# Gate matrices of eight tokens instead of four, one batch per two slabs, with one set of one-hot buffers filled in halves

## What is computed

```python
def block(xt):                                   # 8 heads, 128 x 128 experts, top 16 per head
    q = (xt @ w_q).reshape(T, PEER_HEADS, 2, PEER_HALF)
    s = jnp.einsum('thpd,hpkd->thpk', q, sub_keys)
    s_top, i_top = lax.top_k(s, PEER_TOPK)       # best 16 of each half
    ...                                          # best 16 sums of a pair (i1, i2): eid = i1 * 128 + i2
    gate = jax.nn.softmax(best, axis=-1)
    u_sel, v_sel = jnp.take(u_tab, eid, axis=0), jnp.take(v_tab, eid, axis=0)
    act = jax.nn.gelu(jnp.einsum('td,thkd->thk', xt, u_sel), approximate=False)
    return jnp.einsum('thk,thkd->td', gate * act, v_sel)
```

## Time and profile before

| | us |
|---|---|
| runs, median of 3 | 3200.51 (3197.85 to 3203.13) |
| profiled execution, its own time | 3202.34 |
| its span, first to last instruction | 3200.5 |
| PE busy | 3004.4 (94%) |
| DVE busy | 2184.9 (68%) |
| ACT busy | 1586.0 (50%) |
| POOL busy | 964.1 (30%) |
| gate matmuls (L627), 4608 of them | 200.2 busy |

### The profile page before, as it was taken

How to read it: one execution, slowest core, us unless ns; L and a number is a source line. 1 busy time by engine, 2 the same in 40 slices (tenths; PEclk the granted TensorE clock), 3 DMA queues, 4 the chain that set the end, 5 groups by cost and what they waited for, 6 DMA issues and landing times.

```text
span 3200.5 us, 66478 instructions
## 1 busy us (share of the span) xinstructions
PE 3004.4 (94%) x22938; PEld 2712.0 (85%) x22938; DVE 2184.9 (68%) x4296; ACT 1586.0 (50%) x2568; POOL 964.1 (30%) x377
## 2 busy tenths in 40 slices
PE   7899999999998989999999999688789999999998
PEld 6799999877888879999987778686689999987886
DVE  4379377888555447847788855695629757788755
ACT  3345444676444435544467645343344544467654
POOL 5579600000006567950000000265368940000000
PEclk9899999999999999999999999799899999999999
DMA  5345544455664244554455566233254554445564
GB/s 190 121 167 169 177 158 160 162 164 170 215 195 145 86 147 155 175 171 161 157 165 164 182 204 193 73 118 113 73 167 152 174 171 158 162 160 167 180 191 150
DMA packets 141400, 508.90 MB, mean 159 GB/s; under 512 B 16864, under 2 KB 18016, under 8 KB 140912
## 3 DMA queue, kind: packets, MB, share of 16 engines
q1 hardware_dynamic: 141296, 507.52, 48.3%
HBM read 506.41 MB, written 1.05 MB: 159 GB/s over the span
## 4 chain that ended last, share of the span: by engine, by line
PE 81%; DVE 8%; POOL 4%; issue 3%; ACT 2%; DMA 1%; SPq 0%; ACTq 0%; POOLq 0%; DVEq 0%
PE col L500 13%; PE col L502 12%; PE col L501 12%; PE acc L500 12%; PE acc L501 11%; PE acc L502 11%; POOL w_lo L457 4%; PE acc L627 2%; PE col L627 2%; ACT w_hi L715 1%; DVE work L2046 1%; PE acc L596 1%; DVE h_tok L917 0%; DVE work L1655 0%; DMA ring<-in_v 0%
## 5 line engine op out<-in xcount | busy, mean ns | idle before, releaser
L457 POOL TENSOR_TENSOR w_lo<-ring,w_hi 128x1024 fp32r<-128x1024 f32 x373 | 963.9, 2597 | 1635.3 <-ACT w_hi L715 1632.7
L715 ACT ACTIVATE w_hi<-ring 128x1024 fp32r<-128x1024 f32 x940 | 993.0, 1056 | 602.5 <-PE acc L502 480.0
L500 PE MATMUL col<-x_hi,w_hi 128*128 128x256 f32 (+1 forms) x3968 | 1143.1, 288 | 40.9 <-POOL w_lo L457 32.5
L501 PE MATMUL col<-x_lo,w_hi 128*128 128x256 f32 (+1 forms) x3968 | 1125.8, 284 | 0.0
L502 PE MATMUL col<-x_hi,w_lo 128*128 128x256 f32 (+1 forms) x3968 | 1123.7, 283 | 0.0
L457 DVE TENSOR_TENSOR w_lo<-ring,w_hi 128x1024 fp32r<-128x1024 f32 x567 | 692.4, 1221 | 224.8 <-ACT w_hi L715 224.8
L500 PEld LDWEIGHTS col<-x_hi,w_hi 128*128 128x128 f32 x3968 | 757.0, 191 | 50.4 <-issue 22.0
L502 PEld LDWEIGHTS col<-x_hi,w_lo 128*128 128x128 f32 x3968 | 758.3, 191 | 0.0
L501 PEld LDWEIGHTS col<-x_lo,w_hi 128*128 128x128 f32 x3968 | 753.6, 190 | 0.0
L500 PE MATMUL acc<-w_hi,c_hi 128*128 128x512 f32 x1664 | 668.2, 402 | 16.0 <-DVE c_lo L989 5.8
L501 PE MATMUL acc<-w_lo,c_hi 128*128 128x512 f32 x1664 | 651.1, 391 | 0.0
(11 more groups left out here) (288 smaller groups left out, 2324.5 us busy)
## 6 DMA issues: line engine op xcount, KB each, us to landing
ring<-in_u SPq DMA_DIRECT2D x384, 512.0 KB, 3.2
ring<-in_v SPq DMA_DIRECT2D x384, 512.0 KB, 3.5
ring<-in_wq SPq DMA_DIRECT2D x48, 512.0 KB, 3.2
ring<-in_s_in SPq DMA_DIRECT2D x32, 512.0 KB, 3.5
ring<-in_c_in SPq DMA_DIRECT2D x16, 512.0 KB, 3.2
ring<-in_s_out SPq DMA_DIRECT2D x16, 512.0 KB, 3.5
ring<-in_s_wide SPq DMA_DIRECT2D x12, 512.0 KB, 3.5
ring<-in_ab_in SPq DMA_DIRECT2D x8, 512.0 KB, 6.8
```

Source lines behind the costliest of these rows:

```text
L457: eng.tensor_tensor(k.w_lo[s.slot][:, :], k.ring[s.slot][:, :], k.w_hi[s.slot][:, :].bitcast(F32), ALU.subtract).then_inc(k.lo[s.slot], 1)
L500: pe.matmul(out, a[0], b[0], start=start, stop=False, **kw)
L501: pe.matmul(out, a[0], b[1], start=False, stop=False, **kw)
L715: act.activation(k.w_hi[s.slot][:, :], k.ring[s.slot][:, :], ACT.Copy).then_inc(k.hi[s.slot], 1)
```

## The change

A batch is eight tokens (`GB` = 8), so there are 32 batches a pass, each a burst of 24 gate matmuls that fills a whole bank. TensorE does two slabs, then one burst; at the end slab 62, the last burst, slab 63. `oh1` and `oh2` have one set, of the same bytes as two sets of four tokens before. It is filled in halves: VectorE makes oh1 (all eight tokens in the early pass, the first four in the late one, where ScalarE makes the other four of every batch), then for each half the mask and oh2. The one mask buffer holds four tokens as before, so that the second half's mask waits for the first half's oh2. The one-hots of batch b+1 wait for burst b (before: those of batch n+2 for burst n). Weigh is one instruction of 512 elements for eight tokens instead of two of 256. VectorE's order per two slabs is weigh(b), split_rest(n+4) with coef_rest in the late pass, onehots(b+1), split_rest(n+5) with coef_rest; the split of the fourth slab stands ahead of the first weigh. At the end of an early pass the late pass's onehots(0) follow the last weigh (before: ahead of it). `HEAD` is 10 slabs instead of 4 and the loop has 8 turns of six slabs instead of 9.

```diff
-GB = 4
+GB = 8
 BATCHES = T // GB
-HEAD = BATCHES % UNROLL
-TURNS = BATCHES // UNROLL
-VREST = KEYS - BATCHES
+GATED = 2 * BATCHES
+HEAD = GATED % UNROLL + UNROLL
+TURNS = (GATED - HEAD) // UNROLL
+VREST = KEYS - GATED
...
-        self.oh1_all = sb("onehot_i1", [P, 2, GB, P], BF16)
+        self.oh1_all = sb("onehot_i1", [P, GB, P], BF16)
...
-        self.oh2_all = sb("gated_onehot_i2", [P, 2, PARTS, GB, EARLY], BF16)
+        self.oh2_all = sb("gated_onehot_i2", [P, 2, PARTS, GB // 2, EARLY], BF16)
...
-        self.mask2 = sb("mask_i2", [P, GB, EARLY], BF16)
-        self.gate_all = sb("pairs_of_gate", [P, BATCHES, PARTS, GB, 2], BF16)
+        self.mask2 = sb("mask_i2", [P, GB // 2, EARLY], BF16)
+        self.gate_all = sb("pairs_of_gate", [P, GATED, PARTS, GB // 2, 2], BF16)
...
-            pe.wait_ge(k.oh_ready, b.index() + (g0 + 1))
-            if late and b.base % 2:
-                pe.wait_ge(k.oh1_ready, b.half() + (k.scalar_onehots(layer) + 1))
+            pe.wait_ge(k.oh_ready, b.index() * 2 + 2 * (g0 + 1))
+            if late:
+                pe.wait_ge(k.oh1_ready, b.index() + (k.scalar_onehots(layer) + 1))
...
-            for n in range(HEAD):
+            for n in range(0, HEAD, 2):
                 slab(n)
-                gates(Slab(n), late, wait=n >= SLOTS)
+                slab(n + 1)
+                gates(Slab(n // 2), late, wait=n // 2 >= SLOTS)
...
-            for n in range(BATCHES - UNROLL, BATCHES - 1):
+            for n in range(GATED - UNROLL, GATED, 2):
                 slab(n)
-                gates(Slab(n), late)
-            gates(Slab(BATCHES - 1), late)
-            slab(BATCHES - 1)
+                if n + 2 < GATED:
+                    slab(n + 1)
+                gates(Slab(n // 2), late)
+            slab(GATED - 1)
...
         def onehots(b):
-            act.wait_ge(k.g_full, b.index() + (k.gates_before(layer, 1) - 1))
-            for t in range(GB):
+            act.wait_ge(k.g_full, b.index() + k.gates_before(layer, 1))
+            for t in range(GB // 2, GB):
...
-            if n % 2 and n + 2 < BATCHES:
-                onehots(Slab(n + 2, i))
-            if n + self.AHEAD < BATCHES:
+            if n % 2 and n + 1 < GATED:
+                onehots(Slab((n + 1) // 2, i))
+            if n + self.AHEAD < GATED:
                 coef_lead(s)
...
-        def onehots(b, late, wait=True):
+        def onehots(b, late):
...
-            if b.turn is not None or b.base + g0 > 1:
-                dve.wait_ge(k.g_full, b.index() + (g0 - 1))
+            if b.turn is not None or b.base + g0:
+                dve.wait_ge(k.g_full, b.index() + g0)
...
+            own_tokens = GB // 2 if late else GB
+            shape = [P, own_tokens, P // 2, 2]
+            dve.tensor_tensor(k.oh1[:, 0:own_tokens, :].rearrange("p t (i two) -> p t i two", two=2),
+                              pairs.unsqueeze(1).to_broadcast(shape),
+                              k.i1[:, bass.ds(b.index() * GB, own_tokens), :].unsqueeze(2).to_broadcast(shape),
+                              ALU.is_equal)
...
+            for part in range(2):
+                shape = [P, GB // 2, EARLY // 2, 2]
+                if b.turn is not None or b.base + g0 + part:
+                    dve.wait_ge(k.oh_ready, b.index() * 2 + (2 * g0 + part))
+                dve.tensor_tensor(mask, pairs[:, at // 2:(at + EARLY) // 2, :].unsqueeze(1).to_broadcast(shape),
+                                  k.i2[:, bass.ds(b.index() * GB + part * GB // 2, GB // 2), :].unsqueeze(2)
+                                  .to_broadcast(shape), ALU.is_equal).then_inc(k.mask_ready, 1)
+                dve.wait_ge(k.mask_ready, b.index() * 2 + (2 * g0 + part + 1))
...
+        def early(b, n, i=None):
+            twice = None if i is None else i * 2
+            if n == 0:
+                split_rest(k, dve, Slab(late_u + 3))
+            weigh(Slab(b, i), 0)
+            if b + 1 < BATCHES:
+                split_rest(k, dve, Slab(late_u + n + 4, twice))
+                onehots(Slab(b + 1, i), 0)
+                split_rest(k, dve, Slab(late_u + n + 5, twice))
+            else:
+                onehots(Slab(0), 1)
...
+            if n == 0:
+                value(Slab(first + 3))
+            weigh(Slab(b, i), 1)
+            if b + 1 < BATCHES:
+                value(Slab(first + n + 4, twice))
+                onehots(Slab(b + 1, i), 1)
+                value(Slab(first + n + 5, twice))
```

More of the change, by code:

```diff
@@ L848, in peer @@
             for n in range(HEAD, HEAD + UNROLL):
-                late(n, i * 2)
-        for n in range(BATCHES - UNROLL, BATCHES - 1):
+                late(n, i)
+        for n in range(GATED - UNROLL, GATED - 1):
             late(n)
@@ L1119, in gate_pass @@
         def gate_pass(step):
-            for n in range(HEAD):
-                step(n)
+            for n in range(0, HEAD, 2):
+                step(n // 2, n)
             with dve.Fori(0, TURNS - 1) as i:
-                for n in range(HEAD, HEAD + UNROLL):
-                    step(n, i * 2)
-            for n in range(BATCHES - UNROLL, BATCHES):
-                step(n)
-        for n in range(2):
-            onehots(Slab(n), 0, wait=k.gates_before(layer, 0) + n > 0)
+                for n in range(HEAD, HEAD + UNROLL, 2):
+                    step(n // 2, n, i)
+            for n in range(GATED - UNROLL, GATED, 2):
+                step(n // 2, n)
+        onehots(Slab(0), 0)
         dve.wait_ge(k.evac, k.cols_before[k.first[f"u{layer}"] + EARLY])
@@ L1134, in peer @@
         first = k.first[f"v{layer}"]
-        def early(n, i=None):
-            weigh(Slab(n, i), 0)
-            if n + 2 < BATCHES:
-                onehots(Slab(n + 2, i), 0)
-            elif n + 2 == BATCHES:
+        def early(b, n, i=None):
[8 more added lines that the diff above has]
+            else:
                 onehots(Slab(0), 1)
-            if n < BATCHES - 1:
-                split_rest(k, dve, Slab(late_u + n + SLOTS, i))
         gate_pass(early)
@@ L1147, in peer @@
             self.coef_rest(experts[:, n, :], Slab(first + n))
-        onehots(Slab(1), 1)
         split_rest(k, dve, Slab(first + 2))
@@ L1151, in peer, with late, value @@
         dve.wait_ge(k.evac, k.cols_before[first])
-        def late(n, i=None):
-            weigh(Slab(n, i), 1)
-            if n + 2 < BATCHES:
-                onehots(Slab(n + 2, i), 1)
-            if n < BATCHES - 1:
-                s = Slab(first + n + SLOTS, i)
+        def late(b, n, i=None):
+            twice = None if i is None else i * 2
+            def value(s):
                 split_rest(k, dve, s)
-                if n + SLOTS < BATCHES:
+                if i is not None or s.base < first + GATED:
                     self.coef_rest(experts[:, s.index(first), :], s)
+            if n == 0:
[5 more added lines that the diff above has]
+                value(Slab(first + n + 5, twice))
         gate_pass(late)
-        for n in range(BATCHES, BATCHES + 2):
+        for n in range(GATED, GATED + 2):
             self.coef_rest(experts[:, n, :], Slab(first + n))
@@ L1169, in rest @@
             self.coef_rest(experts[:, s.index(first), :], s)
-        at = first + BATCHES + 2
+        at = first + GATED + 2
         rest(Slab(at))
```

65 lines of the change are left out of this document (26 added, 39 removed).

## The result

The changed kernel takes 3209.75 us (median of 7 runs, 3208.8 to 3213.65), the kernel before 3199.79 (median of 7, 3195.47 to 3203.13): a ratio of 1.0035, 95% interval 1.0023 to 1.0046. It is 10 us slower, where 8.4 us of gain were forecast.

What follows compares the result with a forecast made beforehand. TensorE was taken as the bound (81% of the chain). Terms 7.8 - 0.7 + 1.8 + 7.9 - 3.9 - 4.5 = 8.4 us of gain, from 3200.5 to 3192 us; range 3184 to 3204.

Steps and rivals of the forecast that it cites:

- late loop: Late pass's hardware loop: the one-hot chain makes pairs take 6.37 us against 6.36 now; 72 pairs lose 0.7 us.
- Rival (2): Late loop's chain is longer than summed; slower by over 0.2% if a pair takes 6.58 us; chance 0.15.
- give-back: Late loop: a burst late by d shortens the next chain by d, up to about 0.12 us; d = 0.11.
- Transitions saved: TensorE's early pairs: one burst of 24 instead of two of 12 saves 0.09 us for each of 87: 7.8 us.
- Rival (4): A burst's extra 0.09 us belongs to each 12 matmuls, so 7.8 and 1.8 us of gain go: 3202; chance 0.08.
- Early pair covered: Early pass: next one-hots are ready at P + 5.12, due at P + 6.48 (P: burst's start), so TensorE doesn't wait.
- Late pairs outside the loop: Late pass: 18 pairs outside the loop are ready in time and save 0.10 us each, 1.8 us.
- Starts: Start of each pass: TensorE waits 0.6 us instead of 2.0; gains of 3.15, 3.15 and 1.64 sum to 7.9 us.
- Early ends: End of each early pass: TensorE idles 1.5 us before the last burst; loss 1.3 x 3, 3.9 us.
- Late ends: End of each late pass: TensorE idles 1.7 us before the last burst; total loss 4.5 us.
- Rival (3), the clock: Six new holes of 1.5 to 1.7 us at pass ends slow the clock, 9 us in all: 3201; chance 0.10.

Runs made afterwards that it cites:

- e5: Changed kernel with VectorE's late one-hots ahead of coef_rest, four slabs ahead of the loop, and the turn of TensorE's loop behind a slab: 3179.15 us.
- e10: Changed kernel with four slabs written out ahead of the loop instead of ten, and TensorE's wait in the loop for weigh one batch later: 3208.72 us.
- e3: Changed kernel with the first half's mask ahead of VectorE's oh1 in both passes: 3200.05 us.
- e9: Kernel before the change with ten slabs written out ahead of the loop instead of four: 3205.34 us.
- e8: e7 with ten slabs written out ahead of the loop instead of four: 3179.72 us.
- e6: e5 with VectorE making the last batch's one-hots of each pass ahead of the weigh and splits: 3184.89 us.
- e7: e6 with the late pass's first one-hots behind the two coef_rest and v slab 1's split behind the last weigh: 3175.12 us.

## Why the prediction was wrong

Between the forecast (-8.4) and the sum of the stretches (+11.3) lie 19.7 us: 11.5 in the late loop, 3.6 at the starts, 3.2 behind v slab 64, 1.9 ahead of the u slabs 0 and 1.1 in the early pairs, less 1.7 at the ends. The late loop alone turns the sign, but alone it would give some 3203 (3192 + 11.5), not 3210.

**The step that failed** is the late loop, "6.47 - d = 6.26 + d gives d = 0.11 and a period of 6.37". Rival (2) came true: 6.53, and with 72 pairs 0.7 us lost became 12.2. Link by link, from the rows above:

| link | forecast | measured |
|---|---|---|
| burst to coef_rest | 3.55, less the give-back | 3.45 |
| coef_rest to oh1, to mask | 0.34, 0.33 | 0.34, 0.34 |
| mask to gated one-hot | 0.44 | 0.43 |
| gated one-hot to second mask | 0.70 | 0.74 |
| second mask to gated one-hot | 0.44 | 0.46 |
| gated one-hot to TensorE | 0.61 + 0.06 | 0.78 |
| sum | 6.47 - 0.11 = 6.36 | 6.54 |

The mechanism, the queues and the give-back (Abs at 1.04 behind the burst, as forecast) were right. The size was off by 0.18, 0.11 of it in the last link: the 0.61 came from a pass's start, outside a loop, and it holds there still (381.84 to 382.46 in the changed kernel), but in the loop the same edge takes 0.78. I had added 0.12 for the loop to the edge on VectorE and none to the one that ends on TensorE. The 0.06 there was for TensorE's second semaphore, and that is not what costs: the late pass's last burst waits for it too, outside the loop, and comes 0.62 after its gated one-hot (791.08 to 791.70). The prediction said that 0.2 us more decides the sign; I gave it 0.15 while my sum of nine links could not be good to 0.2. The sum also put the chain exactly at the point where lateness starts to count in full: the give-back of 0.11 was used up, so every further 0.01 cost 0.7 us.

**Transitions saved, 7.8:** measured 6.7. A pair is 6.46 on the mean, 0.02 better than forecast; the turn of the loop, which I did not cost, takes over 0.1 behind a burst of 24. Without it (e5) the stretch gains 9.5. Rival (4) is refuted by this.

**Early pair covered:** right, no wait of TensorE in any.

**Late pairs outside the loop, 0.10 each:** 0.08 each in the five ahead of it (6.28), right.

**Starts, 7.9:** measured 4.3. TensorE's wait was 0.48 (0.6 forecast), the clock stayed at full, and with HEAD = 4 (e10) the three ways come to 3.16, 3.16 and 1.54 against 3.15, 3.15 and 1.64. The change's own part was as forecast. The missing 3.6 came ahead of the gate pass with the longer program, a part of the diff that I named nowhere in the sum; e3, where two layers lack it, shows that it need not come.

**Early ends, 3.9:** 3.5. The last burst came at P + 5.15 (5.12 forecast). **Late ends, 4.5:** 2.9; the last burst came 4.85 after the one before it instead of 5.28, since VectorE was less behind than I had it.

**Rival (3), the clock:** not behind the six holes of 1.1 to 1.4 us. It came behind v slab 70, where 1.18 became 2.09 and the next slabs ran partly at 1.2 GHz. In e3 the hole there is 2.07, the granted clock stayed at 1.00 and the stretch lost 0.8 instead of 2.4, so that the clock took 1.6. The hole itself is 1.09 to 2.27 in the ten experiments, 1.77 in e9 with the batches of before; why it differs stays open, and no experiment bore on it.

## What to carry to other kernels

A batch twice as long saves one switch but halves the number of buffers, and what matters then is the order in each queue: put whatever the bottleneck waits for next ahead of work that waits for a third engine. One exchanged pair of instructions was worth 17 us here, twice what the switches saved in the changed kernel (6.7 early and 1.4 late). Where a forecast chain lies within a few tenths of its due time and is multiplied by 72, give the case that it misses as much chance as the case that it holds, and take each edge from a row in the same kind of place, inside a loop for a loop.

## What was not expected of the hardware

- An edge between engines takes longer in a hardware loop: gated one-hot to TensorE's first matmul 0.62 outside (381.84 to 382.46 early, 791.08 to 791.70 late), 0.78 inside (688.48 to 689.26).
- The turn of TensorE's loop is free behind 12 short matmuls and costs 0.11 us behind 24 in the early pass and 0.07 in the late one; behind a slab it is free again (e5).
- Six more slabs written out went with 0.8 to 2.0 us more a layer in code ahead of them (e8, e9, and e10 the other way), but not in two layers of e3. There, which of VectorE and GpSimd goes first turns on 0.1 us.
- A split on GpSimd held VectorE's bf16 one-hot, 0.68 us alone, to 2.84 (377.85 to 380.69): it ended 0.55 behind the end of the split (380.14), so that nearly all of it came after the split.
- Holes of 1.36 us left the granted clock at 1.00 each time; holes of 2.10 were followed by 0.78 and 0.77 in two layers and 1.00 in the third (e6), one of 2.09 by 0.56, and those of 2.26 and 2.27 at v slab 70 of layer 0 in e6 and e7 by 1.00. So a longer hole was not the surer one.
